# Conditioning sums of a two-layer diffusion trunk: the steps are spread anew over the weight chunks

## What is computed

```
m  = (silu(c)     @ mod_w[i] + mod_b[i])     # 1024 -> 6*1024, latent tokens
mc = (silu(c_ctx) @ mod_w[i] + mod_b[i])     # the same weights, context tokens
h  = modulate(rms_norm(x), m[0], m[1])
p  = h @ w_in[i]                              # 1024 -> all branches and gates
merged = sum over 4 branches of sigmoid(gate_n) * (branch_n @ w_branch[n])
x  = x + m[2] * (merged @ w_o);  h2 = modulate(rms_norm(x), m[3], m[4])
x  = x + m[5] * mixture_of_experts(h2)
```

## Time and profile before

| | us |
|---|---|
| median of three runs | 2329.77 |
| profiled execution, its own time | 2335.57 |
| its span | 2333.8 |
| TensorE busy | 2124.2 (91%) |
| VectorE busy | 1372.8 (59%) |
| ScalarE busy | 991.8 (42%) |
| GpSimd busy | 369.5 (16%) |
| TensorE clock granted, mean | 0.952 of full |

### The profile page before, as it was taken

One profiled execution on the slowest core, in us unless ns is written; L12 is line 12 of the kernel. 1 busy time (PEld: TensorE's weight loads), 2 busy tenths in 40 slices (PEclk: granted clock), 3 DMA queues, 4 the chain that ended last, 5 costly groups with the idle time before them and its releaser, 6 DMA issues.

```text
span 2333.8 us, 28756 instructions
## 1 busy us (share of the span) xinstructions
PE 2124.2 (91%) x10673; PEld 1719.5 (74%) x10673; DVE 1372.8 (59%) x1496; ACT 991.8 (42%) x1290; POOL 369.5 (16%) x400
## 2 busy tenths in 40 slices
PE   5879999999989999978999766999999999889994
PEld 3646788888778888877878654668888878778783
DVE  2655455666766433367989666453344454469885
ACT  3645411321211122227878655442422223348882
POOL 3300000000000001003555323000000000025552
PEclk7979999999989999988999887999999999999997
DMA  7020044444655232029999452003334344269993
GB/s 278 1 63 1 19 122 136 140 123 132 190 175 150 73 109 90 28 107 369 388 362 383 169 197 72 1 1 81 100 87 108 95 122 131 73 254 368 368 371 132
DMA packets 247398, 360.00 MB, mean 154 GB/s; under 512 B 22528, under 2 KB 180480, under 8 KB 245760
## 3 DMA queue, kind: packets, MB, share of 16 engines
q1 hardware_dynamic: 219776, 297.65, 39.0%
q0 software_dynamic: 22336, 42.07, 5.2%
q10 hardware_dynamic: 5184, 18.88, 2.1%
HBM read 354.23 MB, written 36.78 MB: 168 GB/s over the span
## 4 chain that ended last, share of the span: by engine, by line
PE 71%; DVE 12%; DMA 8%; ACT 4%; issue 3%; SPq 1%; POOL 0%; ACTq 0%; DVEq 0%; POOLq 0%
PE ps L641 31%; PE ps L629 17%; PE ps L643 7%; DMA RING<-in_moe_w 4%; PE ps L865 4%; DMA MGZ<-in_mod_w 3%; DVE WS L1754 1%; PE ps L1071 1%; PE ps L824 1%; PE ps L849 1%; PE ps L850 1%; PE ps L851 1%; DVE MGZ L1766 1%; PE ps L813 1%; PE ps L1036 1%
## 5 line engine op out<-in xcount | busy, mean ns | idle before, releaser
L641 PE MATMUL ps<-HTH,WS 128*128 128x512 f32 x1664 | 583.1, 398 | 15.4 <-DVE WS L1754 15.3
L641 PEld LDWEIGHTS ps<-HTH,WS 128*128 128x128 f32 x1664 | 313.7, 189 | 92.8 <-DVE WS L1754 18.7
L641 PE MATMUL ps<-HTL,WS 128*128 128x512 f32 x832 | 328.1, 394 | 0.0
L1302 ACT ACTIVATE WS<-RAWB 128x1024 fp32r<-128x1024 f32 (+1 forms) x128 | 162.7, 1272 | 314.9 <-PE ps L643 109.9
L629 PE MATMUL ps<-HTH,MGH 128*128 128x512 f32 x1000 | 281.1, 404 | 12.1 <-DVE MGH L2122 12.1
L1754 DVE TENSOR_TENSOR WS<-RAWB,WS 128x1024 fp32r<-128x1024 f32 (+1 forms) x128 | 190.5, 1489 | 116.5 <-ACT WS L1302 116.4
L629 PE MATMUL ps<-HTL,MGH 128*128 128x512 f32 x800 | 233.0, 404 | 9.4 <-DVE HTL L2132 9.4
L643 PE MATMUL ps<-HTH,WS 128*128 128x256 f32 x832 | 234.6, 282 | 0.0
L629 PEld LDWEIGHTS ps<-HTH,MGH 128*128 128x128 f32 x1000 | 189.4, 194 | 53.6 <-DVE MGH L2122 8.2
L1527 ACT ACTIVATE HTH<-RING 128x2048 fp32r<-128x2048 f32 x100 | 191.2, 1912 | 77.3 <-DMA RING<-in_moe_w 57.9
L641 PE MATMUL ps<-BRH,WS 128*128 128x512 f32 x512 | 182.6, 397 | 3.5 <-DVE BRL L1910 3.5
(11 more groups left out here) (336 smaller groups left out, 3765.1 us busy)
## 6 DMA issues: line engine op xcount, KB each, us to landing
RING<-in_moe_w SPq DMA_DIRECT2D x300, 512.0 KB, 7.7
RAWB<-in_w_in SPq DMA_DIRECT2D x112, 512.0 KB, 4.2
MGZ<-in_mod_w SPq DMA_DIRECT2D x80, 512.0 KB, 4.0
RAWB<-in_w_branch SPq DMA_DIRECT2D x64, 256.0 KB, 4.8
MGZ<-y_rows POOLq DMA_DIRECT2D x20, 512.0 KB, 6.5
RAWB<-in_w_o SPq DMA_DIRECT2D x16, 512.0 KB, 3.9
HTF<-in_mod_w SPq DMA_DIRECT2D x6, 1024.0 KB, 15.0
h_rows<-BR ACTq DMA_DIRECT2D x10, 512.0 KB, 2.6
```

What stands on the lines that cost most here:

```text
L641: last = mm(psb(pair)[:, 0:SEQ], a[:, k0 + k, :], b[:, k, 0:SEQ], start=go, stop=end)
L1302: act_f(parts(s, words(s))[0], raw_slab(r, words(s)), ACT.Copy).then_inc(S("w_hi"), 1)
```

## The change

One condition in `conditioning_plan` changes, the number of steps that a chunk may get. Before it is three up to chunk 23 and four from chunk 24 on. After, it is four, but two in chunks 24 to 35:

```diff
-        while i < len(ops) and len(plan[s]) < (3 if s < S_CV else 4) and (ops[i][0] // KD < 2 or ops[i][0] // KD - 2 in rows):
+        while i < len(ops) and len(plan[s]) < (2 if S_CV <= s < G_CV else 4) and (ops[i][0] // KD < 2 or ops[i][0] // KD - 2 in rows):
```

## The result

The changed kernel takes 2313.8 us (median of 10 runs, 2308.42 to 2322.59) where the kernel before takes 2329.46 (10 runs beside it). The ratio is 0.9935, interval 0.9920 to 0.9951, so 11 to 19 us faster. The forecast was 2311.4, a gain of 18.4. The profiled execution took 2313.69, with a span of 2311.9. Over all timed runs of this study the means differ by 15.7 us, with 2.1 to either side (17 runs of the changed kernel, 70 of before).

A forecast was written before the change was run, and what follows sets the result against it. TensorE was taken to bound the kernel, stalling where DVE's steps wait for block loads. Gains of 16.4 + 2.5 - 1.1 + 0.6 = 18.4 us from the median 2329.77 gave 2311.4 us, range 2305 to 2320.

The forecast's parts named there:

- What bounds it, and why it stalls: TensorE sets the end; DVE's single-block steps wait for loads in chunks 30 to 33, with lateness reaching chunk 38.
- Part 1: Convolution, chunks 24 to 35: TensorE runs through, b36 starts 16.4 us earlier and takes 2.5 us less at full clock.
- Part 2: Convolution's gate, chunks 36 to 43: six groups of four single steps on DVE cost 1.1 us, 86.1 from b36's end.
- Rivals 1 and 2: Gate not paced by DVE, 2308.4 us, chance 0.15; gate's groups slower, loss 6.8 us, 2317.1, chance 0.15.
- rival 4: Convolution: TensorE still waits as two single blocks a chunk come late at chunks 32 to 35; 3 to 6 us, chance 0.08.
- Part 3: Chunks 0 to 23: four double steps in place of three cost nothing, hidden by TensorE's matmuls.
- Part 4: Chunks 12 to 15, end of the SGU: without three steps ahead of the mixing products, a gain of 0.6 us.
- The sum: Whole kernel: 16.4 + 2.5 - 1.1 + 0.6 = 18.4 us gained, median 2311.4 us.

The follow-up runs named there:

- e2: Kernel before, with the loads of the 32 blocks of halves 6 to 9 left out: chunk 24 to 44 in 208.85 us, median 2317.3 us.
- e3: Changed kernel with four steps a chunk up to chunk 27, two in 28 to 35, three in the gate: stretch 208.75 us, median 2310.3 us.
- e4: Changed kernel with a third slot for the blocks of halves 6 to 9: stretch 208.74 us, median 2312.8 us.
- e8: Changed kernel with a half's eight bias loads issued behind its fourth block, not ahead of its third: stretch 208.74 us, median 2308.7 us.
- e9: Changed kernel without row point 16, four steps a chunk to chunk 28, two in 29 to 35, three in the gate: 208.74 us, median 2312.9.
- e10: Changed kernel with blocks of halves 6 to 9 loaded one ahead, not two: chunk 24 to 44 in 268.56 us, 2371.1 us in all.
- e1: Kernel before with four steps a chunk from chunk 0 on, convolution included: chunk 24 to 44 in 239.03 us, median 2339.8 us.

## Why the prediction was right, step by step

- **What bounds it, and why it stalls.** Right, and shown: leaving out the 32 blocks takes the stall away with all steps in place (e2), and with every load in place fewer steps a chunk (e3) or a third slot (e4) leave TensorE no wait in the stretch. The list of TensorE's waits was not whole. Three of the six for split weights weren't named, 1.12 us ahead of g36, 0.87 ahead of g40 and 0.51 ahead of g41, so the lateness reached beyond chunk 38.
- **Part 1, the convolution.** b36 was to start 121.2 us behind chunk 24 and did at 121.1, in all three profiles. DVE had the convolution's last low part ready 4.2 us ahead of that (at 667.85), where 4.3 were forecast. b36 took 4.28 (4.25). No split was waited for, and there is no half turn between b36 and b37 now: the 1.04 us ahead of g38 went too. With the stall gone, the granted clock stayed at 1.00.
- **Part 2, the gate.** 86.1 was expected, 86.04 to 86.40 measured. The waits ahead of g39, g41 and g43 were forecast at 0.9, 0.8 and 0.8 and are 0.9, 0.6 and 1.3 (1.0, 1.0 and 0.7, then 1.0, 1.1 and 0.9 in the other two profiles). g40 and g42 don't wait. That the total agrees within 0.1 us is in part luck. The six groups took 9.6, 8.5, 9.5, 9.0, 9.5 and 9.7 us, where 9.6, 8.5, 9.6, 8.5, 9.6 and 10.3 were forecast. The last one was 0.6 shorter (9.1 and 10.1 us in the other two profiles), split 44 was ready at 85.4, and TensorE, not DVE, set the start of chunk 44. The 0.4 us forecast ahead of it didn't come, and g43's longer wait made up for most of that. Rivals 1 and 2 fall, by 3 and by 6 us, and with part 1 rival 4, since two single blocks a chunk came in time. The Trainium skill's fit for a load ("SBUF — State Buffer", The DMA setup-cost knee) gives an estimate of 3.2 us for a block. The trace doesn't agree: the 40 loads of blocks in this stretch of the changed kernel took 3.6 us at the least and 3.9 in the median, and the groups kept to the longer time.
- **Part 3, chunks 0 to 23.** Right. The steps wait for a block once, 1.5 us, as before. Half 0's turn stands at chunk 5 and not at 7, and nothing else moves: from chunk 12 to chunk 15 it is 28.02 us, 28.03 before.
- **Part 4, the SGU.** Half seen rightly. ACT writes the second high part at 438.27, ahead of chunk 15's end (441.88), so its 0.8 us are out of the way, but the split for chunk 17 still stands between chunk 15 and the last unit. From chunk 15's end to g16 it is 3.83 us, 4.31 before: 0.5, where 0.6 was forecast.

```profile
438.27 0.85 ACT L1305 ACTIVATE BRH<-T 128x768 fp32r<-128x768 f32 x1 [1.01 <-DVE T L1888]
442.12 1.48 ACT L1302 ACTIVATE WS<-RAWB 128x1536 fp32r<-128x1536 f32 x1 [3.01 <-PE ps L643]
```

- **The sum.** In the trace: mean stretch 229.1 less 211.6 is 17.5 (17.8 forecast), and 0.5 in the SGU (0.6), 18.0 together (18.4 forecast). Timed: 15.7, with 2.1 to either side. The mechanism and its size in the stretch are as forecast. Of the 2.3 us between 18.0 and 15.7 I can't say whether they are scatter or real. They are not in the profiled executions, which differ by more: 2311.1 and 2333.9 on the mean of three, 22.8 us. Of these, 5.2 lie behind chunk 44, where the change touches nothing and where kernels with the same work took 1545 to 1556 us, so I count none of it as gain. No run here looks into an execution that isn't profiled.

**Versions that beat both.** e3, e4, e8 and e9 all take 208.7 us in the stretch, TensorE's own time for the work. Their 22 runs, on two chips, have a mean of 2311.4, the changed kernel's 17, on all chips, of 2314.7. The difference, 3.3 us with 2.6 to either side, agrees with the 2.8 in the trace. e8 is the smallest edit: it moves eight tiny loads. In this stretch nothing more is to be had from spreading steps, since TensorE has no idle time left in it.

## What to carry to other kernels

Count transfers, not only work, when small steps are spread over a schedule: with two slots, two transfers a stage are free, and the next ones can only start when a slot comes free inside the stage. Here the third block of a group cost DVE a wait of some 2.4 us and the fourth 0.7 to 2.8 us more (median 1.2), and not a whole load each, since the two loads overlap (a group of 8.5 us for 5.1 us of steps). With bias loads ahead of the third, the wait for it was up to 5.0. With one block ahead (e10) nothing overlaps, and each block cost a whole load, 3.8 to 4.0 us. The stage must be long enough to hide this. Put groups that need many transfers where the stage is long, and groups that reuse a transfer where it is short. Where the engine is last by a microsecond or so, a slot more, one step less or a few small loads moved out of the queue's way each give the same, so take the cheapest.

## What the hardware showed that I had not expected

**The clock's fall has no fixed price.** The same stall in three executions of the kernel before: chunks 34 and 35 took 11.20 and 8.47, 9.83 and 11.02, 10.92 and 10.15 us (8.48 undisturbed), behind idle times of 5.23 and 3.04, 5.21 and 4.72, 4.71 and 3.74. Their granted clocks were 0.73 and 1.00, 0.85 and 0.76, 0.77 and 0.83. The stretch differed by only 0.7 us all the same, and the rows fit DVE setting the pace there: a slow chunk ended in a shorter wait, and chunk 34 with the wait behind it made 14.2, 14.6 and 14.7 us. In e10 an idle time of 1.80 us was followed by a chunk of 10.01 us at 0.83, while in e1 the chunk behind one of 1.11 us kept a granted clock of 1.00 and took 8.6 us.

**TensorE has two paces at a full clock.** With no idle time, g1 takes 8.48 us to b0 in the first and third profiles of both kernels, and 8.32 in the second of both, and b0 to b7 is 80.56 or 79.04 before, 81.75 or 80.64 after (with one half turn more inside). From the first gate product to the end of b7 that makes 1.9 us before and 1.4 after, independent of the change. Both paces also stand in one execution: in e1 g20 took 8.32 us and g23 8.48, at a granted clock of 1.00. This is the reason why whole stretches from the first gate product are poor evidence for a gain of one microsecond. What decides the pace is open.
